# Filling TensorE's waits with products that nobody reads, and moving the conditioning sums of a dense FFN

## The reference, cut to what matters

```
for layer in (0, 1):
    mod = c @ w_ada[layer] + b_ada[layer]            # six vectors of 1024: shifts, scales, gates
    mix = concat(retention, state space, window attention)(x * (1 + sc_a) + sh_a) @ w_out
    x = layer_norm(alpha * x + (1 + g_a) * mix)
    h = x * (1 + sc_f) + sh_f
    f = dense FFN(h) if layer == 0 else mixture of 8 experts(h)   # top 2 by router logits h @ w_router
    x = layer_norm(alpha * x + (1 + g_f) * f)
```

## Time and profile before

| | |
|---|---|
| median of 3 runs | 2714.97 us (2712.18 to 2715.39) |
| the profiled execution | 2711.7 us, its span 2709.9 us |
| TensorE busy | 2618.8 us, 97% of the span |
| VectorE busy | 2191.4 us, 81% |
| ScalarE busy | 1525.4 us, 56% |
| TensorE's mean granted clock | 0.985 |
| mean transfer rate | 247 GB/s |

### The profile page before, as it was taken

The page is one execution under the profiler, slowest core; times in us unless marked ns, Lnnn a source line. Parts: engine busy times, 40 slices in busy tenths (PEclk is TensorE's granted clock), DMA queues, the critical chain, the costliest instruction groups (busy, mean ns, idle before and its releaser), DMA issues.

```text
span 2709.9 us, 37744 instructions
## 1 busy us (share of the span) xinstructions
PE 2618.8 (97%) x15664; PEld 2330.4 (86%) x15664; DVE 2191.4 (81%) x2459; ACT 1525.4 (56%) x1576; POOL 50.8 (2%) x83
## 2 busy tenths in 40 slices
PE   6989999989999999999999999999999999999998
PEld 5869988878888888888888799998899999988898
DVE  6977877788989898988989889875487788954777
ACT  3533335557767777777777755444544555344544
POOL 2010000000000000000000000000000000000000
PEclk9989999989999999999999999999999999999999
DMA  8659964489999999999999953444555533444453
GB/s 317 223 191 335 354 228 156 127 313 367 353 352 363 351 361 354 368 343 360 352 360 360 324 182 123 142 166 140 175 195 188 170 121 133 156 163 164 157 186 116
DMA packets 376000, 669.85 MB, mean 247 GB/s; under 512 B 26761, under 2 KB 199439, under 8 KB 370959
## 3 DMA queue, kind: packets, MB, share of 16 engines
q1 hardware_dynamic: 358336, 662.55, 69.5%
q10 hardware_dynamic: 17487, 4.83, 0.7%
HBM read 663.13 MB, written 4.19 MB: 246 GB/s over the span
## 4 chain that ended last, share of the span: by engine, by line
PE 79%; DVE 12%; ACT 4%; issue 3%; DMA 1%; ACTq 0%; POOL 0%; DVEq 0%; SPq 0%; POOLq 0%
PE PS L445 23%; PE PS L447 22%; PE PS L446 22%; DVE LO L440 4%; DVE AR L2824 3%; PE PS L545 2%; DVE AR L722 2%; ACT HI L431 2%; PE PS L2534 2%; PE PS L1674 2%; PE PS L1911 1%; PE PS L2573 1%; PE PS L2410 1%; PE PS L2590 1%; PE PS L750 0%
## 5 line engine op out<-in xcount | busy, mean ns | idle before, releaser
L440 DVE TENSOR_TENSOR LO<-RAW,HI 128x2048 fp32r<-128x2048 f32 x410 | 930.0, 2273 | 209.1 <-ACT HI L431 208.7
L431 ACT ACTIVATE HI<-RAW 128x2048 fp32r<-128x2048 f32 x410 | 780.0, 1903 | 306.7 <-PE PS L447 268.2
L445 PE MATMUL PS<-X1H,HI 128*128 128x256 f32 (+1 forms) x2128 | 611.9, 288 | 9.9 <-DVE X1L L585 4.2
L446 PE MATMUL PS<-X1L,HI 128*128 128x256 f32 (+1 forms) x2128 | 605.7, 285 | 0.0
L447 PE MATMUL PS<-X1H,LO 128*128 128x256 f32 (+1 forms) x2128 | 605.6, 285 | 0.0
L445 PEld LDWEIGHTS PS<-X1H,HI 128*128 128x128 f32 (+1 forms) x2128 | 409.5, 192 | 15.8 <-issue 13.0
L445 PE MATMUL PS<-HI,X1H 128*128 128x512 f32 x1056 | 420.7, 398 | 1.5 <-DVE LO L440 0.4
L447 PE MATMUL PS<-HI,X1L 128*128 128x512 f32 x1056 | 412.7, 391 | 0.0
L446 PE MATMUL PS<-LO,X1H 128*128 128x512 f32 x1056 | 412.6, 391 | 0.0
L446 PEld LDWEIGHTS PS<-X1L,HI 128*128 128x128 f32 (+1 forms) x2128 | 409.5, 192 | 2.2
L447 PEld LDWEIGHTS PS<-X1H,LO 128*128 128x128 f32 (+1 forms) x2128 | 409.4, 192 | 1.1
(11 more groups left out here) (393 smaller groups left out, 2821.5 us busy)
## 6 DMA issues: line engine op xcount, KB each, us to landing
RAW<-in_w_in_dram SPq DMA_DIRECT2D x66, 1024.0 KB, 5.4
RAW<-in_expert_w_gate_dram SPq DMA_DIRECT2D x66, 1024.0 KB, 6.2
RAW<-in_expert_w_up_dram SPq DMA_DIRECT2D x64, 1024.0 KB, 6.4
RAW<-in_expert_w_down_dram SPq DMA_DIRECT2D x62, 1024.0 KB, 6.0
RAW<-in_ffn_w_up_dram SPq DMA_DIRECT2D x55, 1024.0 KB, 5.7
AR<-in_expert_w_down_dram SPq DMA_DIRECT2D x50, 1024.0 KB, 6.8
AR<-in_expert_w_up_dram SPq DMA_DIRECT2D x48, 1024.0 KB, 6.3
AR<-in_expert_w_gate_dram SPq DMA_DIRECT2D x46, 1024.0 KB, 5.5
```

The costliest lines, as they stand in the source:

```text
L431: a.activation(HI[:, n % NH, 0:size(i)], raw_at(i), ACT.Copy).then_inc(*hi.up(i))
L440: v.tensor_tensor(LO[:, m % NH, 0:n], raw_at(i), HI[:, m % NH, 0:n].bitcast(F32), ALU.subtract).then_inc(*lo.up(i))
L445: t.matmul(o, lh, rh, start=first, stop=False)
L446: t.matmul(o, lh, rl, start=False, stop=False)
```

## The change

It has five parts. (1) A function `keep_clock(t, bank, n)` issues n float32 products of 256 columns into a PSUM bank, whose result nobody reads; they stand in TensorE's queue before waits: 4 at the start of mixer 1 (with a wait for ScalarE's first copy of the memory columns), 3 after `y(0)` in both mixers, 4 after `pe_ada_sum` 2, 6 at the start of the dense FFN, 6, 4 and 5 in the router, 6 before the FFN of the last layer. (2) The router's logits take 128 columns in place of 8, of which 8 are read; WR becomes wider, and GpSimd clears the added columns once. (3) The denominators of the mLSTM take 128 columns in place of 1. (4) In the FFN, VectorE's `done` splits the chunk first and reads sums 3 and 4 one chunk sooner (n = 9 and 18); TensorE's sums 5 and 6 move from n = 28 to n = 30, and VectorE reads them after the last pair's hidden values. (5) `before_end` is called between the second and third bank of the last `mm_down_pair` instead of before it, and waits for sum 5, which is read last.

```diff
@@ -249,7 +249,8 @@
     MOD = sb("MOD", [128, 2, 48])
     BT = sb("BT", [128, 4, 256])
     SM = sb("SM", [128, 640])
-    WR = sb("WR", [128, 8, 8])
+    WRP = sb("WR", [128, 184])
+    WR = WRP[:, 0:64].rearrange("p (c n) -> p c n", c=8)
     PPT = sb("PPT", [128, 256], F32R)
     PS = ctx.enter_context(nc.psum_tensor("PS", [128, 8, 512], F32))
 
@@ -475,9 +476,11 @@
                     z = piece(c, q // 2, q % 2)
         return z
 
-    def mm_down_pair(t, pair, LH, LL, banks, finished):
+    def mm_down_pair(t, pair, LH, LL, banks, finished, between=None):
 
         for q in range(4):
+            if between:
+                between(q)
             ts, ns = slice(128 * (q // 2), 128 * (q // 2) + 128), slice(512 * (q % 2), 512 * (q % 2) + 512)
             for n, i in enumerate(pair):
                 for c in range(2):
@@ -560,6 +563,11 @@
             turn(t, [(PS[:, b, 256 * ci + 128 * tt:256 * ci + 128 * tt + 128],
                       src[:, tt, 128 * (2 * cp + ci):128 * (2 * cp + ci) + 128])
                      for ci in range(2) for tt in range(2)]).then_inc(*pe_fm.up(tag, cp))
+
+    def keep_clock(t, bank, n):
+
+        for _ in range(n):
+            t.matmul(PS[:, bank, 0:256], ident, CST[:, C_ONE:C_ONE + 256], start=True, stop=True)
 
     def fm_bank(banks, cp, ci):
         return PS[:, banks[cp % len(banks)], 256 * ci:256 * ci + 256]
@@ -1003,6 +1011,9 @@
         if l == 0:
             t.wait_ge(*xin.all())
             t.wait_ge(*act_front("bias", 3))
+        if l:
+            t.wait_ge(*act_fm("mem", 0))
+            keep_clock(t, 0, 4)
         pe_to_fm(t, ("h", l), X, [4, 5], (lambda nb: dve_res("z", 0, 1, nb)) if l else None)
         ready = lambda q: dve_fm(("h", l), "lo", q)
         rows = lambda j, k: pe_gemm_blk(t, f"in{l}r{j}", k, X1H, X1L, [0, 1], ready)
@@ -1172,6 +1183,7 @@
         pe_rows(t, (l, 0), MOD[:, l, 16:24])
         t.wait_ge(*dve_mix("gate", l, 1))
         y(0)
+        keep_clock(t, 2, 3)
         turn_mix(0)
         y(1)
         turn_mix(1)
@@ -1194,6 +1206,7 @@
             pe_rows(t, "gate", MOD[:, 1, 40:48])
         else:
             pe_ada_sum(t, 2, 2)
+            keep_clock(t, 3, 4)
         pair = CH[f"out{l}"][2:]
         for n in range(2):
             t.wait_ge(*lo(pair[n]))
@@ -1587,13 +1600,12 @@
                     done(n, p)
                     n += 1
             if p == N_PAIRS and paired:
-                before_end()
                 pair = CH[key + "d"][N_PAIRS - 2:]
                 for q, i in zip(downs(p), pair):
                     t.wait_ge(*lo(i))
                     t.wait_ge(*dve_ffn(key, "lo", q))
                 mm_down_pair(t, pair, lambda n, c: RH3[:, (N_PAIRS - 2 + n) % 3, c, :],
-                             lambda n, c: RL3[:, (N_PAIRS - 2 + n) % 3, c, :], [4, 5, 6, 7], key + "d").then_inc(
+                             lambda n, c: RL3[:, (N_PAIRS - 2 + n) % 3, c, :], [4, 5, 6, 7], key + "d", before_end).then_inc(
                     *used.up(pair[1]))
             for q in downs(p) if p < N_PAIRS or not paired else ():
                 i = CH[key + "d"][q]
@@ -1699,19 +1711,21 @@
 
     def pe_ffn1(t):
         def done(n, p):
-            if n in (9, 18, 28):
+            if n in (9, 18, 30):
                 t.wait_ge(*dve_ffn("ffn", "hid", p - 1))
                 pe_ada_sum(t, 2 + n // 9, 2 * ((p + 1) % 2))
-            if n == 28:
+            if n == 30:
                 pe_ada_sum(t, 6, 2 * ((p + 1) % 2), 16)
 
-        def before_end():
-            t.wait_ge(*dve_ada("mod", 6))
-            t.wait_ge(*dve_ffn("ffn", "hid", N_PAIRS - 1))
-            pe_late_params(t, 0)
-            pe_late_params(t, 1)
-            pe_rows(t, (0, 1), MOD[:, 0, 40:48])
-
+        def before_end(q):
+            if q == 2:
+                t.wait_ge(*dve_ada("mod", 5))
+                t.wait_ge(*dve_ffn("ffn", "hid", N_PAIRS - 1))
+                pe_late_params(t, 0)
+                pe_late_params(t, 1)
+                pe_rows(t, (0, 1), MOD[:, 0, 40:48])
+
+        keep_clock(t, 3, 6)
         pe_to_fm(t, ("f", 0), X, [2, 3], lambda nb: dve_res("z", 0, 0, nb))
         pe_ffn(t, "ffn", ("f", 0), lambda p: act_ffn("ffn", "silu", p) if p not in (2, 5) else dve_ada("mod", 3 + p // 3),
                lambda p: dve_ffn("ffn", "hid", p), done, before_end, True)
@@ -1744,9 +1758,9 @@
 
     def dve_ffn1(v):
         def done(n, p):
-            if n in (10, 19):
+            split_lo(v)
+            if n in (9, 18):
                 dve_ada_sum(v, 2 + n // 9, 2 * ((p + 1) % 2))
-            split_lo(v)
             if n < 28:
                 ada_step(v, ADA1 + n)
 
@@ -1771,11 +1785,11 @@
             if p in (1, 2):
                 dve_gains(v, 0, 0, p - 1)
         split_lo(v)
+        hidden(N_PAIRS - 1)
+        split_lo(v)
         dve_ada_sum(v, 6, 2, 16)
         dve_ada_sum(v, 5, 2)
         dve_combine(v, 0, 1)
-        hidden(N_PAIRS - 1)
-        split_lo(v)
         split_lo(v)
         dve_memory(v)
         dve_residual(v, 0, 1, "ffnd", lambda: None)
@@ -1808,19 +1822,23 @@
             turn(t, [(PS[:, cp, 256 * ci + 128 * tt:256 * ci + 128 * tt + 128],
                       X[:, tt, 128 * (2 * cp + ci):128 * (2 * cp + ci) + 128])
                      for ci in range(2) for tt in range(2)]).then_inc(*pe_moe.up("xf", cp))
+        keep_clock(t, 4, 6)
         t.wait_ge(*act_moe("xf", 3))
         t.wait_ge(*misc.all())
+        t.wait_ge(*pool_mix("wide"))
         for k in range(2):
             for c in range(8):
-                z = t.matmul(PS[:, 0, 8 * k:8 * k + 8], XF[:, c, 128 * k:128 * k + 128], WR[:, c, :], start=(c == 0),
-                             stop=(c == 7))
+                z = t.matmul(PS[:, 0, 128 * k:128 * k + 128], XF[:, c, 128 * k:128 * k + 128], WRP[:, 8 * c:8 * c + 128],
+                             start=(c == 0), stop=(c == 7))
         z.then_inc(*pe_moe.up("logits"))
+        keep_clock(t, 2, 4)
         t.wait_ge(*dve_moe("picked"))
         t.matmul(PS[:, 1, 0:8], tri, RK[:, 0, :], start=True, stop=True)
         t.matmul(PS[:, 1, 8:16], ones, RK[:, 0, :], start=True, stop=False)
         t.matmul(PS[:, 1, 8:16], tri, RK[:, 1, :], start=False, stop=True)
         t.matmul(PS[:, 1, 16:24], ones, RK[:, 0, :], start=True, stop=False)
         t.matmul(PS[:, 1, 16:24], ones, RK[:, 1, :], start=False, stop=True).then_inc(*pe_moe.up("ranked"))
+        keep_clock(t, 3, 5)
 
     def act_router(a):
         a.wait_ge(*dve_res("combined", 1, 0))
@@ -1848,7 +1866,7 @@
             v.wait_ge(*pe_moe("xf", cp))
         dve_gains(v, 1, 0, 0)
         v.wait_ge(*pe_moe("logits"))
-        v.tensor_tensor(LGT, PS[:, 0, 0:16].rearrange("p (k n) -> p k n", k=2), view(rbias, [0, 2], [1, 8]),
+        v.tensor_tensor(LGT, PS[:, 0, 0:256].rearrange("p (k n) -> p k n", k=2)[:, :, 0:8], view(rbias, [0, 2], [1, 8]),
                         ALU.add).then_inc(*dve_moe.up())
         v.wait_ge(*dve_moe.last())
         mine, other = view(LGT, [8, 2], [1, 8], [0, 8]), view(LGT, [8, 2], [0, 8], [1, 8])
@@ -2499,9 +2517,10 @@
         def values():
             t.wait_ge(*dve_two("weights", 3, l))
             for h in range(4):
-                t.matmul(PS[:, 2, h:h + 1], EE[:, h, 0:128], ones[:, 0:1], start=True, stop=True)
-                t.matmul(PS[:, 2, 4 + h:5 + h], EE[:, h, 128:256], ones[:, 0:1], start=True, stop=False)
-                z = t.matmul(PS[:, 2, 4 + h:5 + h], EE[:, h, 256:384], ones[:, 0:1], start=False, stop=True)
+                t.matmul(PS[:, 2, h:h + 128], EE[:, h, 0:128], ones, start=True, stop=True)
+            for h in range(4):
+                t.matmul(PS[:, 2, 4 + h:132 + h], EE[:, h, 128:256], ones, start=True, stop=False)
+                z = t.matmul(PS[:, 2, 4 + h:132 + h], EE[:, h, 256:384], ones, start=False, stop=True)
             z.then_inc(*pe_two.up("den", l))
             for h in range(4):
                 val = lambda k: VT[:, k, 256 * h:256 * h + 256]
@@ -2595,6 +2614,8 @@
         if l == 0:
             t.wait_ge(*act_two("memory", "next"))
             pe_keys(t, CH["ek"][3], MF, 2)
+        else:
+            keep_clock(t, 2, 6)
 
         pe_to_fm(t, ("nf", l), XN, [4, 5, 6, 7], lambda nb: dve_two("normed", nb, "ffn", l))
         key = f"ff2{l}"
@@ -3174,6 +3195,7 @@
             pool_rsqrt(g, RS[:, k:k + 1], MV[:, k, 1:2], LN_EPS, "res", l, j, k)
 
     def gpsimd_program(g):
+        g.memset(WRP[:, 64:184], 0.0).then_inc(*pool_mix.up("wide"))
         g.memset(MHALF, -0.5).then_inc(*pool_rs.up("minus_half"))
         g.wait_ge(*pool_rs.last())
         pool_rotary(g)
```

## The result

| | before | changed |
|---|---|---|
| median | 2713.57 us (4 runs, 2711.38 to 2715.39) | 2695.68 us (4 runs, 2694.06 to 2698.44) |
| the profiled execution; its span | 2711.7; 2709.9 | 2695.19; 2693.4 |
| TensorE's mean granted clock | 0.985 | 0.994 |
| TensorE busy | 2618.8 us | 2615.3 us |

Changed over before: 0.9933, 95% interval 0.9919 to 0.9947, so 18.2 us less (14.4 to 22.0). Forecast were 2702 and -12.7.

A forecast was written before the change was run, and what follows sets the result against it. TensorE was taken as the bound: its work, its unabsorbed waits and the 1.2 GHz stretches behind them. Terms summed to -12.7 from the profiled 2711.7, giving 2699.0; plus 3.3 for the median, 2702 us, range 2696 to 2711.

The forecast's parts named there:

- Mixer 0: Unread products in mixer 0's waits keep the clock up and bring w_out's last chunk sooner: -3.4 us, bounds -1.6 to -3.4.
- Starts of the FFN and of mixer 1: Unread products before transposes waiting for normalised X gain 0, since VectorE covers it; bounds 0 to -0.5 us each.
- Order in the FFN: New order of sums in the FFN removes TensorE waits, its end gives some back: -4.2 us, bounds -7.7 and -1.5.
- Sums 5 and 6: In the FFN, moved behind later chunks, they lose their 2.95 us wait and slow clock: 4.3 us gained.
- sums 3 and 4: In the FFN, reading them a chunk sooner shortens TensorE's waits: 0.9 us gained at the first, 0.88 at the second.
- rival (b): The FFN's new order gives nothing: VectorE bounds the stage and waits return at the next meeting; 2706.5 us, chance 0.2.
- Mixer 1: Three unread products behind `y(0)`, with no wait ahead, lie on the path: +1.2 us, bounds 0 and 1.3.
- Router: Start stays; logit products gain 1.0 us and the gather 2.05 at the upper clock: -3.0 us, bounds -3.0 and -1.0.
- Denominators: 128 columns in the mLSTM cost little and end the slow stretch behind them: -2.8 us over two layers, bounds 0 and -3.0.
- Rival (a): Wherever waits are filled, the clock falls nonetheless, as unread products don't count or other gaps suffice; 2713 us, chance 0.12.
- Rival (c): In router, mixers and end, unread products run at 1.2 GHz and outlast their waits: +6.2 us, 2721, chance 0.04.
- The rule on transposes: Skill page: transposes don't count as busy, so the clock could fall in the router's first ones; its 3.0 us lost, 2705.

The follow-up runs named there:

- c_more_starts: Changed kernel with 10 instead of 6 unread products at the FFN's start and 9 instead of 4 at mixer 1's; 2696.3 us, ratio 0.9923.
- a3_order_only: Kernel before with only the FFN's new order and the later `before_end` call; 2708.01 us, ratio 0.9977.
- d_step_first: Changed kernel with VectorE's step 48 put ahead of the split of the same turn; 2692.2 us, ratio 0.9922.
- d_end_sooner: Changed kernel with the late transposes and gate's rows behind the first of the last four banks instead of the second; 2695.05 us, ratio 0.9936.

## Why the prediction was right in most of its steps and wrong in its number

**Mixer 0** (-3.4, measured -3.6). From the end of the wait of `turn_mix(0)` to the first product behind `gated(1)` it took 146.15 - 140.39 = 5.76 against 5.70 in mixer 1 before, and the gain was carried through w_ada's loads to the pair of w_out, as argued: ScalarE begins on the last chunk of w_out at 162.38 instead of 164.34, 1.96 sooner against the 1.75 forecast. One thing came otherwise: the clock fell at 161.6, ahead of the four unread products, which ran at 0.50. They still ended inside the wait, so it cost nothing.

**Starts of the FFN and of mixer 1** (0). More unread products there (`c_more_starts`) change nothing that can be measured. In the changed kernel's profile, though, neither term is 0: 0.9 us are lost behind the first start, where the low stretch ends 2.1 us later in the stage than before (192.3 against 193.8, in a stage that begins 3.6 sooner), and 0.5 are won behind the second, whose low stretch lasts 6.8 us instead of 10.2. The rows of the FFN and of mixer 1 contain them.

**Order in the FFN** (-4.2, measured -3.3 in the changed kernel, -5.7 alone). Sums 5 and 6 gave more than their 4.3: the time from where TensorE began to wait (373.67 - 2.95) to the first product behind the sums (380.68 in the same timeline) was 9.96, now it is 383.41 - 378.14 = 5.27, that is 4.7. The end gave back 1.4 (4.7 less the stage's 3.3) instead of 1.9; VectorE's last sum begins 397.93 - 383.41 = 14.5 after the first of the four banks, against the 14.7 forecast. But sums 3 and 4, which were to bring 1.8, brought 0.9 in the changed kernel, as much as the start had lost: the wait of 0.88 went, the wait of 2.95 came back as 2.93 on step 48, as rival (b) had it, and with it the fall of the clock, at 262.1 before and at 304.8 now. Alone, in `a3_order_only`, they brought 2.5: a wait of 2.54 came back there, but neither fall. `d_step_first` shows that it was again a wait for an order and not for VectorE's capacity.

**Mixer 1** (+1.2, measured +0.7). The three products are on the path and cost 1.3, as forecast; the rest is the 0.5 won at the stage's start. Whether they are a loss depends on the fall that they hold off, 1.6 us in 3 of 9 profiles without them. By these counts they cost some 0.8 us more than they save (an estimate: 1.3 - 3/9 x 1.6).

**Router** (-3.0, measured -2.7). The start stays, the logits take 3.7, the gather 3.8. The gather ends 3.2 sooner, of which 0.5 is lost again because the experts' first product now waits 0.26 us for VectorE's X1L. That the part alone measures -5.7 is not the router's doing as far as its profile shows: 2.7 there, and 3.2 from two low stretches in the second block that this execution lacks. In other executions of the kernel before the router's low stretch is longer (to 569.3), which would add 1.6.

**Denominators** (-2.8, measured -3.3). Widening cost next to nothing: the twelve products took 1705.24 - 1702.65 = 2.59 before and 1694.22 - 1691.55 = 2.67 now (starts of the first of them and of the next group), 0.08 more where the prediction had 0.2. The first of them before, and the two groups now:

```profile
1702.65 0.28 PE L2502 MATMUL PS<-CST,AR 128*128 128x1 f32 x2
```

```profile
1691.55 1.05 PE L2520 MATMUL PS<-CST,AR 128*128 128x128 f32 x8
...
1694.22 0.60 PE L2527 MATMUL PS<-AR 128*128 128x256 f32 x2
```

The Trainium skill, "TensorE: Matmul & The Clock Gate", section "Back-to-back issue gap", gives a record of 128 columns more than twice the cycles of one of a single column; the measurement decides, and here the growth is 3%.

**The step that failed** is the base of the sum: it is made "against the profiled execution's 2711.7", and "3.3 above it" is added for the median. Every low stretch that no part of the change touches was thereby taken to stay, at no term and without a reason, above all the two ahead of the denominators, near 1692 and 2259. They were worth -3.0 in the two profiles. The forecast was 6.6 us above the measured median, in two pieces:

- 3.8 in the sum. 3.0 of these are the two stretches ahead of the denominators. The kernel before has them in all of four profiles, the changed kernel in 2 of 8 places. At 1.5 each that is 6/4 x 1.5 = some 2.3 us per execution (an estimate from these counts), a gain that nobody wrote into the change. The rest is small and of both signs: experts 0.7, mixer 1 and denominators 0.5 each, mixer 0 0.2 and the end 0.1 more than forecast, FFN 0.9 and router 0.3 less. That the sum up to the experts came out so close (-8.9 against -9.4) is in part luck, since it is made of misses of both signs: in the FFN alone +0.9 at its start, +0.9 at sums 3 and 4, -0.4 at sums 5 and 6, -0.5 at its end.
- 2.8 in the conversion. The first profile of the kernel before lay 3.3 under the median shown, that of the changed kernel 0.5 under its own. The profiles of one kernel differ (2710.85 to 2715.2 for the kernel before; of the 3.5 us between the first and the second, 3.2 are two low stretches), so this distance was itself a draw and not to be carried over.

The same holds for the parts: alone, the denominators, the order and the router measured 1.8, 2.0 and 2.7 more than their terms. Each interval still holds its term; that of the whole (14.4 to 22.0) does not hold 12.7. Rival (a) did not come about, but for the one fall at 146.0 in `d_end_sooner`. Rival (c) came about in part, in mixer 0: four unread products took 2.84 us behind a fall, and fitted in the wait even so; in the router four of them take 1.89 us, as at the upper clock, and nothing started late. (b) was right about the first wait, though the bound was again an order, and wrong about the whole. The rule on transposes, by which the router's 3.0 would be lost, is not borne out: 2.7 came. What stands ahead of the prediction calls these transposes plain products with the identity. That is not shown: the kernel calls `t.transpose`, and each leaves one record where a plain float32 product leaves two.

**What stays open.** Why the same wait brings a fall in one execution and not in the next, and why the changed kernel has so many fewer of them ahead of the denominators. The wide denominators can't be the cause in layer 0, since they come behind this place. Chance alone with one rate for all kernels fits badly with 11 of 12 against 8 of 22. The moment at which the wait comes remains as a candidate, and it is only argued: of the two delays that were to test it, one moved the wait by 0.4 us and the other by 2.1, with one profile each. A delay at a place where no wait takes it up, in several profiles, was not tried.

## What to carry to other kernels

Unread products in a wait pay where the wait is the only gap and TensorE is next in demand; where another engine paces what follows, they pay nothing. The falls behind this kernel's longer waits (mixer 0, router, end) were in every profile that left the wait as it was; those at waits of 0.8 to 1.2 us, and the length of some, differed from one execution to the next. So profile the unchanged kernel several times before a sum is built on its low stretches, and give places with short waits a share, not a yes or no. Give a share also to low stretches that the change doesn't touch. When a wait comes back at the next meeting, look at the order on the engine that is waited for before calling it the bound: one swapped step took 3.5 us by the medians and 4.5 in the profile.

## What the runs showed of the hardware

- One program, the same instructions and the same waits (0.82 and 1.18 us), granted 0.50 in one execution and 1.00 in another. Where TensorE has work all through it, a single low stretch of 3.4 us costs 1.5 to 1.7 us; over a wait it costs nothing that shows (161.6 in the changed kernel). Over the kernel before's timed runs the mean granted clock goes from 0.982 to 0.987, and the time with it from 2719.8 to 2708.5.
- Float32 products of 128 columns took 3% longer than those of one column (2.67 against 2.59 us for twelve, the same in four profiles of each kernel).
- Products that nobody reads, issued ahead of a wait, keep the upper clock behind it: behind the router's and the last layer's waits in 25 of 25 places with them, and in none of 15 without.
